# Attention masks of the dilated-window layer: added by TensorE instead of VectorE, with the phase's four instruction streams put in a new order

## The reference, cut to what matters

```
s = jnp.einsum('bthd,btnhd->bthn', q, kg).astype(f32) * (HEAD_DIM ** -0.5)
s = s + bias_tab[rel_bucket(n * dil)].astype(f32).T
s = jnp.where(valid[:, None, :], s, -jnp.inf)
lse = jax.nn.logsumexp(s, axis=-1)
p = jnp.exp(s - lse[..., None])
o = jnp.einsum('bthn,btnhd->bthd', p, vg.astype(f32))
```

## Time and profile before

| | |
|---|---|
| median of three runs | 2049.85 us |
| the profiled execution | 2052.1 us |
| its span, first to last instruction | 2049.9 us |
| PE busy | 1904.6 us, 93% |
| DVE / ACT / POOL busy | 58% / 47% / 24% |
| mean granted TensorE clock | 0.971 |
| the attention phase of layer 1 | 667.8 to 742.1 us |

### The profile page before, as it was taken

The page is one execution under the profiler, slowest core; times in us unless marked ns, Lnnn a source line. Parts: engine busy times, 40 slices in busy tenths (PEclk is TensorE's granted clock), DMA queues, the critical chain, the costliest instruction groups (busy, mean ns, idle before and its releaser), DMA issues. The chain is left out here.

```text
span 2049.9 us, 37623 instructions
## 1 busy us (share of the span) xinstructions
PE 1904.6 (93%) x14714; PEld 1806.9 (88%) x14714; DVE 1182.0 (58%) x2049; ACT 959.7 (47%) x1570; POOL 489.8 (24%) x511
## 2 busy tenths in 40 slices
PE   6899988999999989999897869999998999799999
PEld 4899987999999679999885649999998999699998
DVE  4667774555444456554446765555475787555544
ACT  3666663444333334443433554443356666444432
POOL 3122221244200313431103202343211221024420
PEclk9899998999999999999999999999998999899999
DMA  6357765655565746555648715654563776456554
GB/s 176 110 190 227 232 191 143 169 164 157 155 193 169 213 126 166 165 153 165 207 134 283 286 43 169 169 164 141 158 191 103 232 232 211 126 162 170 164 145 134
DMA packets 501689, 353.09 MB, mean 172 GB/s; under 512 B 14741, under 2 KB 486215, under 8 KB 500739
## 3 DMA queue, kind: packets, MB, share of 16 engines
q1 hardware_dynamic: 493644, 304.97, 51.4%
q0 software_dynamic: 7440, 45.43, 5.9%
q10 hardware_dynamic: 430, 0.29, 0.1%
HBM read 327.03 MB, written 50.63 MB: 184 GB/s over the span
## 5 line engine op out<-in xcount | busy, mean ns | idle before, releaser
L268 PE MATMUL ps<-xh,whi 128*128 128x288 f32 x2368 | 655.7, 303 | 9.8 <-PEq L176 9.6
L240 DVE TENSOR_TENSOR wlo<-raw,whi 128x2048 fp32r<-128x2048 f32 (+3 forms) x241 | 501.9, 2083 | 248.4 <-ACT whi L229 248.3
L268 PE MATMUL ps<-xl,whi 128*128 128x288 f32 x2368 | 645.1, 299 | 0.0
L229 ACT ACTIVATE whi<-raw 128x2048 fp32r<-128x2048 f32 (+3 forms) x241 | 419.1, 1740 | 268.1 <-PE ps L276 231.1
L268 PEld LDWEIGHTS ps<-xh,whi 128*128 128x128 f32 x2368 | 452.9, 191 | 12.0 <-issue 10.2
L268 PEld LDWEIGHTS ps<-xl,whi 128*128 128x128 f32 x2368 | 453.8, 192 | 0.8
L276 PE MATMUL ps<-xh,wlo 128*128 128x288 f32 x2368 | 353.3, 300 | 0.0
L276 PEld LDWEIGHTS ps<-xh,wlo 128*128 128x128 f32 x2368 | 327.2, 189 | 1.1
L520 POOL TENSOR_TENSOR gh<-sg,ut 128x288 f32<-128x288 f32 x88 | 216.2, 2457 | 353.1 <-ACT sg L461 353.1
L268 PE MATMUL ps<-hh,whi 128*128 128x288 f32 x704 | 189.7, 296 | 0.0
L268 PE MATMUL ps<-hl,whi 128*128 128x288 f32 x704 | 189.6, 297 | 0.0
(11 more groups left out here) (320 smaller groups left out, 2667.7 us busy)
## 6 DMA issues: line engine op xcount, KB each, us to landing
raw<-in_ffn_w_in SPq DMA_DIRECT2D x176, 512.0 KB, 5.0
raw<-in_ssm_w_in SPq DMA_DIRECT2D x80, 512.0 KB, 4.9
raw<-in_ffn_w_out SPq DMA_DIRECT2D x64, 384.0 KB, 4.0
raw<-in_ffn_w_out SPq DMA_DIRECT2D x64, 320.0 KB, 3.2
H<-in_state_ssm SPq DMA_DIRECT2D x32, 512.0 KB, 7.5
out_ssm_sample<-H SPq DMA_DIRECT2D x32, 512.0 KB, 6.5
raw<-in_ssm_w_out SPq DMA_DIRECT2D x32, 512.0 KB, 5.0
Kp_L<-in_cache_diff_k SPq DMA_DIRECT2D x64, 256.0 KB, 4.7
```

Of the source, the lines that this page charges most:

```text
L229: act.activation(wts["hi"][:, s, 0:width], raw[:, s, 0:width], ACT.Copy).then_inc(hi_ready.sem, 1)
L240: dve.tensor_tensor(wts["lo"][:, s, 0:width], raw[:, s, 0:width], wts["hi"][:, s, 0:width].bitcast(F32), ALU.subtract).then_inc(lo_ready.s ...
L268: pe.matmul(out, W[0][:, kk, j, :], x_[:, k, :], stop=False, start=(part == 0 and kk == 0 and x_ is seg.hi), skip_group_check=True)
```

## The change

The mask is no longer 128 rows that DVE adds, but 4 rows (one for each token of a sequence) with 128 more columns that say which output row belongs to which token. `tables_` multiplies these columns by the 4 rows and accumulates on the one-hot product: every table matmul gets a second one behind it. The result in PSUM is then final: ACT copies the old keys' 896 columns to `bias`, and DVE copies the 12 new ones.

All loads of the table now count on one semaphore, `loaded`: `rb` four times, `barred`, `oh` (in this order on SP). Both `lay_tables` on DVE and `tables_` on PE wait for all six. In `lay_tables` this was a wait for `rb` alone.

The calls are put in another order on PE, ACT and DVE, and `order` with them.

```diff
-            oh, barred = scratch[:, 0:N_OLD + 12], scratch[:, 1024:1024 + N_OLD + 12]
+            oh, barred = scratch[:, 0:N_OLD + 12], scratch[0:T, 1024:1024 + N_OLD + 12 + P]
...
-                     + keys_of(1, 1, 0, 8) + turned_of(6) + [("out", 0, 0), ("out", 0, 1)] + turned_of(7)
+                     + keys_of(1, 1, 0, 8) + [("out", 0, 0), ("out", 0, 1)] + turned_of(6) + turned_of(7)
...
-                    sp.dma_start(rb[32 * t:32 * t + 32, :], A["rel_bias"]).then_inc(rows_in.sem, rows_in.inc())
+                    sp.dma_start(rb[32 * t:32 * t + 32, :], A["rel_bias"]).then_inc(loaded.sem, loaded.inc())
+                sp.dma_start(barred, A["barred_swa"]).then_inc(loaded.sem, loaded.inc())
                 sp.dma_start(oh, A["onehot_swa"]).then_inc(loaded.sem, loaded.inc())
-                sp.dma_start(barred, A["barred_swa"]).then_inc(masks_in.sem, masks_in.inc())
...
                     pe.wait_ge(laid.sem, laid.at(8))
-                    pe.wait_ge(loaded.sem, loaded.at(1))
+                    pe.wait_ge(loaded.sem, loaded.at(T + 2))
...
-                        mm = pe.matmul(out, LT[:, g, :], oh[:, lo:lo + n], start=True, stop=True)
+                        pe.matmul(out, LT[:, g, :], oh[:, lo:lo + n], start=True, stop=False)
+                        mm = pe.matmul(out, barred[:, N_OLD + 12:], barred[:, lo:lo + n], start=False, stop=True)
...
                 keys(0, 0, 3, 6)
+                unit_exp(1)
+                act.wait_ge(tables.sem, tables.at(1))
+                act.activation(bias[:, 0:N_OLD], flat[:, 2560:2560 + N_OLD], ACT.Copy).then_inc(mixed.sem, mixed.inc())
                 keys(0, 0, 6, 8)
-                unit_exp(1)
...
                     dve.wait_ge(filled.sem, filled.at(1))
-                    dve.wait_ge(rows_in.sem, rows_in.at(T))
+                    dve.wait_ge(loaded.sem, loaded.at(T + 2))
...
-                def bar_keys():
+                def lay_new_keys():
                     dve.wait_ge(tables.sem, tables.at(1))
-                    dve.wait_ge(masks_in.sem, masks_in.at(1))
-                    dve.tensor_tensor(bias[:, 0:N_OLD], flat[:, 2560:2560 + N_OLD], barred[:, 0:N_OLD], ALU.add).then_inc(
-                        mixed.sem, mixed.inc())
-                    dve.tensor_tensor(base[:, :], ps[:, 7, 0:12], barred[:, N_OLD:], ALU.add).then_inc(
-                        laid.sem, laid.inc())
-
-                def lay_new_keys():
+                    dve.tensor_copy(base[:, :], ps[:, 7, 0:12]).then_inc(laid.sem, laid.inc())
...
-    barred = np.tile(parts[32] * np.float32(NEG), (P // T, 1)).astype(np.float32)
+    barred = np.concatenate([parts[32] * np.float32(NEG), i[None] % T == t], axis=1).astype(np.float32)
```

More of the change, by code:

```diff
@@ L2004, in swa @@
             filled, laid, tables, mixed = S("buffers_filled"), S("tables_laid"), S("bias_tables"), S("bias_moved")
-            new_bias, rows_in, masks_in = S("new_bias"), S("bias_rows_loaded", 16), hankel_in
+            new_bias = S("new_bias")
             staged, half_out = S("out_staged"), o_moved
@@ L2213, in _ @@
                 unit_scores(1)
-                turn(0, 0, 3, 8)
+                turn(0, 0, 3, 6)
                 tables_()
                 unit_scores(2)
+                turn(0, 0, 6, 8)
                 unit_turn(0)
@@ L2219, in _ @@
                 unit_values(0)
+                unit_scores(3)
                 turn(0, 1, 0, 3)
                 unit_turn(1)
-                unit_scores(3)
                 unit_values(1)
+                unit_scores(4)
                 turn(0, 1, 3, 6)
                 unit_turn(2)
-                unit_scores(4)
                 unit_values(2)
@@ L2234, in _ @@
                 unit_turn(4)
+                unit_values(4)
                 turn(1, 0, 4, 8)
-                unit_values(4)
                 turn_probs(0)
@@ L2240, in _ @@
                 unit_turn(5)
+                unit_values(5)
                 unit_scores(7)
-                unit_values(5)
                 scores_wide(1)
@@ L2245, in _ @@
                 scores_rest(1)
+                turn_out(0)
                 unit_turn(6)
-                turn_out(0)
                 unit_values(6)
@@ L2435, in _ @@
                 keys(0, 0, 0, 3)
+                lay_queries()
                 lay_tables()
-                lay_queries()
                 unit_lowest(1)
-                keys(0, 0, 3, 8)
                 unit_scale(0)
-                bar_keys()
+                keys(0, 0, 3, 6)
                 unit_lowest(2)
+                lay_new_keys()
+                keys(0, 0, 6, 8)
                 unit_scale(1)
-                lay_new_keys()
+                unit_lowest(3)
                 unit_out(0)
@@ L2447, in _ @@
                 unit_scale(2)
-                unit_lowest(3)
+                unit_lowest(4)
                 unit_out(1)
                 keys(0, 1, 3, 6)
-                unit_lowest(4)
                 unit_scale(3)
@@ L2458, in _ @@
                 unit_lowest(5)
-                keys(1, 0, 0, 8)
+                keys(1, 0, 0, 4)
                 unit_out(4)
+                keys(1, 0, 4, 8)
                 move(dve, copy, "prob", 0, 1)
```

## The result

| | before | after |
|---|---|---|
| median | 2049.11 us (4 runs, 2046.49 to 2052.1) | 2064.45 us (4 runs, 2061.4 to 2067.58) |
| ratio, 95% interval | | 1.0076 [1.0056, 1.0095] |
| the profiled execution | 2052.1 us | 2056.42 us |
| its attention phase of layer 1 | 72.36 us | 86.79 us |

The kernel is 15.3 us slower; 7.9 were forecast. (The profiled execution of the changed kernel is not among its four; all seven on record lie between 2056.4 and 2068.1.) The direction was right, the time lies above the range.

What follows compares the result with a forecast made beforehand. PE, busy 93% of the span, was taken to bound the kernel. Head +4.6, middle +1.95 and tail +1.35 gave +7.9 us, so 2049.85 became 2057.8 us, range 2052 to 2062.

Steps and rivals of the forecast that it cites:

- the size of the tables: Table matmuls on PE at the head: 3.36 us plus 2.6 for the added ones, 5.95 in all.
- +1.2 us as the bound: Table matmuls on PE: the most added if the low clock, taken as about 3.5 us of work, lasts until they end.
- rival 3: Low clock stays on through the tables, with a late one-hot landing: +10.3 us, 2060.2; chance 0.15.
- The wait of 1.25 us before `scores_wide(0)`: End of the head: PE waits 1.25 us for DVE's copy of key piece 7.
- The load's landing: One-hot load `oh`, issued on SP at 671.18, lands at 675.05 and ends DVE's new wait.
- `LT`'s start: DVE in the head: `LT` runs from 675.1 to 676.1, after the wait for the one-hot load.
- PE's idle stretch: PE ahead of the tables: idle for 3.7 us from 672.5, which brings the low clock.
- the tables' start: PE in the head: tables start at 676.2, about when they did before (676.40).
- Rival 2: One-hot load lands early, by 673.4, clock stays full: +4.65 us, 2054.5; deciding landing about 674; chance 0.15.
- Middle and tail: After the head: PE waits, mostly for `PTu` between turn and values of a unit, +1.95 and +1.35 us.
- the wait of 0.74 us before `scores_rest(0)`: Middle of the phase on PE: 0.27 us of waiting there was to go and was subtracted.
- Rival 1: The handovers in middle and tail are hidden and only the head costs: +4.6 us, 2054.5; chance 0.15.

Runs made afterwards that it cites:

- e1: Changed kernel, but the added matmuls use full 128-row weights (LT by the one-hot columns again, mask left out); 2056.65 us, 1.0036 of the kernel before.
- e2: Changed kernel with the six one-hot matmuls first, then the six mask matmuls; 2059.77 us, 1.0056 of the kernel before.
- e4: Changed kernel without the added mask matmuls, new waits and order kept; 2054.14 us, 1.003 of the kernel before.
- e12: Kernel before with one-hot load ahead of bias rows, key piece 3 copied before LT, plus the new mask in alternating matmuls; 2052.81 us, 1.0017.
- e13: Changed kernel, but the added matmuls use 64 rows of LT and the one-hot matrix, mask left out; 2064.86 us, 1.0074 of the kernel before.
- e6: Changed kernel with the old 128-row mask, its DVE addition and the old wait, so the new order alone; 2051.53 us, 1.0014 of the kernel before.
- e3: Changed kernel, but LT on DVE waits for the bias rows alone, PE for mask and one-hot load; 2060.27 us, 1.0052 of the kernel before.
- e5: Kernel before with the new mask alone (alternating matmuls, DVE copies the result), old order and wait; 2056.57 us, 1.0026 of the kernel before.
- e11: Same as e12, but the six one-hot matmuls first, then the six mask ones, one start flag per bank; 2048.09 us, 0.9992 of the kernel before.
- e10: Kernel before with the one-hot load issued first by ACT, and DVE copying key piece 3 before LT; 2044.76 us, 0.9981 of the kernel before.

## Why the prediction was wrong

**The step that failed** is the size of the tables, "1.7 us" for the two wide ones, "1.3" for the small: 5.95 us in sum. They took 10.85, which is 4.9 of the 6.5 us by which the phase was missed. The step had two things wrong.

The first is the price of a matmul. It was priced by its columns, from rows in which one kind of weights follows its like: the earlier trace rows has 128-row passes among 128-row ones and 33-row passes among 33-row ones. From these it concluded that few rows are not cheaper, which holds, but not that two row counts in turn are dearer. e1, e2, e4, e12 and e13 show that: at the low clock 0.30 us for each of the six wide matmuls and 0.09 for each of the six small ones, 2.3 us of the 10.85. The old trace does show it, in rows that the forecast used for something else. In the earlier trace rows the three 64-row matmuls at 686.20, between 128-row ones, take 0.86 us to the next start, while six passes of 128 columns at the forecast's own 0.11 are 0.67. And the load of such weights starts with them, at 679.76 (see the earlier trace rows for the matmuls), not ahead of them:

```profile
679.76 0.74 PEld L2182 LDWEIGHTS ps<-QKV_L 64*128 64x128 f32 x6
```

The second is the clock: forecast low for about 3.5 us, with +1.2 us as the bound if it stayed low until the end of the tables. It was low for 17.1, so the tables' columns ran at half speed to the last. By the forecast's own prices the twenty short passes are 2.6 us at full clock, so the same again at half of it: the bound should have been +2.6. 5.95 with 2.6 and 2.3 is the 10.85 measured. Why the clock stayed low for so long is open (see the last section).

The Trainium skill, TensorEngine Tiling (Array Packing), section Key Properties, has a rule that may bear on this and that the forecast passed over: changing the tiling mode, not just the tile, drains the engine. The page does not say whether weights with another row count are such a change, and gives no price. The traces look like it: the load of such weights begins only as the matmul before ends (672.28).

**The low clock behind the tables** gave `unit_scores(2)`, the two pieces, `unit_turn(0)` and `scores_wide(0)` another 2.7 us together that the forecast did not have (0.72, 0.78, 0.56 and 0.62, by their steps against 0.86, 0.98, 0.86 and 1.85). It is rival 3 in kind, low through the tables, but with these 2.7 and the 2.6 within the tables the clock cost 5.3 us where that rival gave it 1.2.

**The wait of 1.25 us before `scores_wide(0)`** did not appear. Counted from the phase's start, DVE's key copy was forecast to end at +18.2 and PE to arrive at +17.0. The copy ended at +23.5, since DVE's work ahead of it waits for the tables and `unit_scores(2)` too, and PE came at +23.7. So the missing wait hides 1.25 us of the other errors: with faster tables, in e6, it is there, 2.32 us.

**The load's landing** was forecast as 3.9 us after its issue; in the kernels where a wait shows it, it took 3.3 to 5.1. `LT`'s start, PE's idle stretch (3.7 forecast, 3.44 measured) and the tables' start (+8.13 in the phase, 8.35 forecast) came as said. Rival 2 is out for this profile. In e4 the load landed at +5.6 in the phase, ahead of that rival's point of +6.15; PE was idle for 2.02 us only, and the clock fell for 6.8 us all the same.

**Middle and tail**, forecast +3.3: the waits that came are 0.58, 1.20, 0.64, 0.63, 0.63, 0.18 and 0.63, those that went 0.67 and 0.20, in sum +3.62. Each named wait stands where it was put, at its size within 0.3 us; only the wait of 0.74 us before `scores_rest(0)`, of which 0.27 was to go, did not change. Rival 1 is out.

**The range** was too narrow because its upper end rested on rival 3, whose worst case had the low clock end with the tables. The bound took for granted that a busy PE gets its clock back soon, as it did after the idle stretch in the old phase. (The prediction gives its sum once as +7.8 and else as +7.9; nothing hangs on that.)

## What to carry to other kernels

Price a matmul with its neighbours: weights with another row count than the matmul before have their load in the open (0.20 us at full clock, 0.30 at the low one, 0.09 with 4 columns), so of accumulating matmuls first all of one row count, then all of the other, or pad the few rows. And compare steps only at the same granted clock. The mask's addition on DVE, beside a full TensorE, cost PE nothing here; moved to TensorE it costs its columns, and maybe the clock behind it. When a wait is taken off one engine, look for who needs the same data next: in e3 the wait only moved to PE.

## What the runs showed of the hardware

- A busy PE can fall to the low clock. e5 (10.2 us from 677.9), e12 (3.4 from 681.5) and e11 (6.8 from 679.1) fell in or just behind the added matmuls, when PE had not been idle for at least 3.9 us. The three kernels in which 24 alternating passes follow an idle stretch of 3.2 to 4.1 us (after, e3, e13) stayed low for 17.1 us each; with full rows (e1, 3.6 us idle) or without the mask (e4, 2.0 us idle) it was 6.8.
- What in that stream does it stays open. Exposed loads don't explain e11, which has none within its groups (e2, grouped too, was low for a second time from 678.1, with PE busy). Few rows would explain all of these, if 64 of 128 count as few (e13). But neither is needed: twelve of the fourteen traces have falls like that of 1733.5 in the SSD layers, 23 in all, where PE stood for at most 0.4 us of the 13 before and 15 or 16 passes of 4 columns with weights of 128 rows had just run. So passes of few columns are a third candidate, and the added matmuls double them. They don't suffice either: e1 runs twelve of them at full clock and stays there. With one profile of each it is not settled, and no run varied the columns.
- The issue of four small loads on SP took 1.7 to 3.3 us in these traces, all ahead of the one-hot load in the kernel before. That, and 3.3 to 5.1 us of landing, is what e10 hides by issuing it first and elsewhere.
